# First projection of a fused transformer kernel: the first two weight units run together behind the norm's tiles, and GpSimd splits the second unit's weights right after the first's

## The reference

```python
def first_block(x, c, ...):
    x = layer_norm(x, ln_in_g, ln_in_b)
    c_act = jax.nn.silu(c)
    mod = c_act @ w_ada[l] + b_ada[l]            # 6 vectors of 1024
    sh1, sc1, gt1, sh2, sc2, gt2 = split(mod, 6)
    h = x * (1.0 + sc1) + sh1
    proj = h @ w_in[l]                           # 1024 x 1952
    q_c, kv_c, k_r, r_q, r_k, r_v, r_g = split(proj, IN_OFFSETS)
    a = mla_mixer(...); r = retention_mixer(...)
    y = concatenate([a, r]) @ w_out[l]
    ...                                          # norm, feed-forward, norm
```

## Time and profile before

| | |
|---|---|
| median of 3 runs | 2508.26 us (2506.33 to 2508.92) |
| the profiled execution | 2505.62 us |
| its span | 2503.8 us, so 1.8 us lie around it |
| mean granted clock of PE | 0.987 |
| busy PE, PEld | 95%, 75% of the span |
| busy DVE, POOL, ACT | 56%, 30%, 25% of the span |

### The profile page before, as it was taken

The page is one execution under the profiler, slowest core; times in us unless marked ns, Lnnn a source line. Parts: engine busy times, 40 slices in busy tenths (PEclk is TensorE's granted clock), DMA queues, the critical chain, the costliest instruction groups (busy, mean ns, idle before and its releaser), DMA issues.

```text
span 2503.8 us, 28798 instructions
## 1 busy us (share of the span) xinstructions
PE 2370.2 (95%) x11364; PEld 1889.9 (75%) x11364; DVE 1396.0 (56%) x1618; ACT 626.2 (25%) x943; POOL 761.7 (30%) x513
## 2 busy tenths in 40 slices
PE   6999889999999999999998799998998999999998
PEld 3777566667678888888886478886586788879977
DVE  7567764435633553454445879998528320337733
ACT  4012244432522112101123621213204210024520
POOL 1231330025562332333355122410246223240021
PEclk9999989999999999999999899999999999999999
DMA  6652000032242332333232121111132531110021
GB/s 234 200 183 79 22 20 9 9 119 84 62 119 75 111 96 83 98 107 99 80 106 78 31 101 48 34 42 51 42 118 84 170 86 45 50 34 18 2 93 76
DMA packets 227108, 200.42 MB, mean 80 GB/s; under 512 B 15040, under 2 KB 202816, under 8 KB 225968
## 3 DMA queue, kind: packets, MB, share of 16 engines
q1 hardware_dynamic: 221808, 172.06, 22.8%
q10 hardware_dynamic: 3840, 21.89, 2.2%
q0 software_dynamic: 1344, 4.91, 0.5%
HBM read 173.79 MB, written 17.83 MB: 77 GB/s over the span
## 4 chain that ended last, share of the span: by engine, by line
PE 77%; DVE 9%; issue 4%; ACT 4%; PEld 2%; DMA 1%; POOL 1%; PEldq 1%; SPq 0%; ACTq 0%; DVEq 0%; POOLq 0%
PE G L1741 28%; PE G L308 25%; PE M L3182 3%; PE G L1172 2%; PE M L315 2%; PE G L2678 2%; PE M L1776 1%; PE M L2680 1%; POOL WL L285 1%; PE M L3159 1%; PE M L1123 1%; PE M L1057 1%; DVE MMX L1389 1%; PE G L1152 1%; PEldq L3349 1%
## 5 line engine op out<-in xcount | busy, mean ns | idle before, releaser
L282 POOL TENSOR_SCALAR WH<-RAW 128x1024 fp32r<-128x1024 f32 (+1 forms) x156 | 134.1, 859 | 873.2 <-PE G L1741 453.9
L308 PE MATMUL G<-HH,WH 128*128 128x512 f32 x1024 | 321.0, 395 | 14.5 <-POOL WL L285 4.3
L308 PE MATMUL G<-HL,WH 128*128 128x512 f32 x1024 | 316.8, 391 | 0.0
L308 PE MATMUL G<-HH,WL 128*128 128x512 f32 x1024 | 316.5, 390 | 0.0
L285 POOL TENSOR_TENSOR WL<-RAW,WH 128x1024 fp32r<-128x1024 f32 (+1 forms) x156 | 302.1, 1936 | 13.0
L308 PEld LDWEIGHTS G<-HH,WH 128*128 128x128 f32 x1024 | 191.0, 189 | 59.1 <-issue 13.8
L308 PEld LDWEIGHTS G<-HH,WL 128*128 128x128 f32 x1024 | 193.1, 189 | 40.7
L308 PEld LDWEIGHTS G<-HL,WH 128*128 128x128 f32 x1024 | 193.0, 188 | 40.7
L1741 PE MATMUL G<-HH,WH 128*128 128x512 f32 x608 | 208.4, 394 | 4.7 <-POOL WL L285 4.7
L1741 PE MATMUL G<-HH,WL 128*128 128x512 f32 x608 | 205.5, 389 | 0.0
L1741 PE MATMUL G<-HL,WH 128*128 128x512 f32 x608 | 205.4, 389 | 0.0
(11 more groups left out here) (583 smaller groups left out, 4441.8 us busy)
## 6 DMA issues: line engine op xcount, KB each, us to landing
RAW<-in_w_ff SPq DMA_DIRECT2D x40, 512.0 KB, 3.8
RAW<-in_w_ff SPq DMA_DIRECT2D x80, 256.0 KB, 2.8
WVEC<-in_w_ada SPq DMA_DIRECT2D x24, 512.0 KB, 4.6
FVEC<-in_e_w_mod SPq DMA_DIRECT2D x24, 512.0 KB, 4.0
FVEC<-in_o_w_mod SPq DMA_DIRECT2D x24, 512.0 KB, 3.7
RAW<-in_o_w_in SPq DMA_DIRECT2D x24, 512.0 KB, 3.7
RAW<-in_e_w_in SPq DMA_DIRECT2D x20, 512.0 KB, 3.6
ADA<-in_w_ada SPq DMA_DIRECT2D x4, 2048.0 KB, 18.4
```

The lines of the kernel that those rows point to most:

```text
L282: pool.tensor_scalar(hi, raw, 1.0, 0.0, ALU.mult, ALU.add).then_inc(w_high, 1)
L308: m = pe.matmul(G[s][:, n * w:(n + 1) * w], part[s][:, k, :], acts[i][:, k, n * w:(n + 1) * w], start=first, stop=last)
```

## The change

The lead of "win" becomes a function of its own, `win_lead`: for each tile k it waits for `li_lo`, then issues the 6 matmuls of unit 0 into G0 and the 6 of unit 1 into G1. `win_pe` starts with unit 2. POOL waits for `ada_added` once, at unit 0, and splits unit 1's weights right after unit 0's; DVE's second increment of `ada_added` goes.

```diff
@@ start_dve
                 low(f)
                 low(f + 1)
-            dve.wait_ge(S("li_lo"), KT)
-            dve.sem_inc(ada_added, 1)
@@
+        def win_lead(pe):
+            u0 = info("win")["u0"]
+            for k in range(KT):
+                pe.wait_ge(S("li_lo"), k + 1)
+                for s in range(2):
+                    if k == 0:
+                        pe.wait_ge(w_split[s], u0 // 2 + 1)
+                        need(pe, unit_freed[s], u0 // 2)
+                    for part, a in ((WH, HH), (WH, HL), (WL, HH)):
+                        first, last = k == 0 and part is WH and a is HH, k == KT - 1 and part is WL
+                        for n in range(2):
+                            m = pe.matmul(G[s][:, half(n)], part[s][:, k, :], a[:, k, half(n)], start=first, stop=last)
+                    if k == KT - 1:
+                        m.then_inc(unit_done[s], 1)
+
         def win_pe(pe):
             for j in range(16):
-                if j:
+                if j >= 2:
                     gemm_unit(pe, j % 2, (u0 + j) // 2, SEQ, (HH, HL))
@@ win_pool
             for j in range(16):
-                if j < 2:
-                    pool.wait_ge(ada_added, j + 1)
+                if j == 0:
+                    pool.wait_ge(ada_added, 1)
                 split_one(pool, r0 + j, u0 + j, KT)
@@
-        stage("win", dict(lead=lead_in("win", SEQ, "li_lo"), act=win_act, pe=win_pe, dve=win_dve, sp_free=win_sp,
+        stage("win", dict(lead=win_lead, act=win_act, pe=win_pe, dve=win_dve, sp_free=win_sp,
```

## The result

The changed kernel took 2524.21 us (median of 4 runs, 2521.45 to 2525.88) against 2508.59 us for the kernel before in the same comparison: a ratio on record of 1.0052, 95% interval 1.0038 to 1.0066, so 9.5 to 16.6 us slower (13.0 in the middle). This ratio is not the quotient of the two medians, which is 1.0062 or 15.6 us; no run tells why, and the other ratios of this document differ from the quotient of their medians in the same way, by up to 0.0010. The forecast was 2519.5 in a range of 2514.5 to 2523.0. The direction, the place and the mechanism were right. The size was short: by the median 4.7 us, which puts the median 1.2 us above the range; by the ratio, put on the 2508.3 that the forecast started from, the time is 2521.3, which is 1.8 us above the forecast and inside the range.

The account below looks back on a forecast made before the run. TensorE, busy 95% of the 2503.8 us span, was taken as the bound. Gate 12.1, relief -1.4 and restart +0.8 made +11.5 us on 2508.3, so 2519.8, rounded down to 2519.5; range 2514.5 to 2523 us.

Parts of the forecast that it names:

- The mechanism: Gate behind the lead: opens after 96 matmuls instead of 48, delaying WVEC, unit 0's copy and unit 2; +12.1 us.
- The early split at the port: Start of the lead: GpSimd's split and VectorE's norm operations take turns, so TensorE starts 2.3 us late.
- the one played through: Order at the port: t32(0), GpSimd's first split operation, t32(2), GpSimd's subtraction, then low(0), ending at 52.4 us.
- The lead: Units 0 and 1 together, 96 matmuls: TensorE never waits after the first tile, and the lead ends at 76.4 us.
- The relief: Between gate and unit 2: unit 3's 512 KB load no longer travels with WVEC's, 1.4 us off the 11.86.
- The restart: Unit 2 after 10.6 us idle: lower clock loses 2.0 us; with unit 4's wait filled, net +0.8 us.
- After unit 4: Rest of the stage: copies wait for TensorE, not WVEC; loads, splits and stages follow TensorE's pace.
- The sum: Whole kernel: gate 12.1, less 1.4 relief, plus 0.8 restart, gives +11.5 us.
- VectorE keeps ahead at the port: Rival, chance 0.28: same gate, but the lead starts only 0.4 us late; +9.3 us, 2517.6 us.
- The gate costs nothing that counts: Rival, chance 0.05: WVEC's rows early or later waits swallow the delay; unit 2 waits for its split; no change, 2508.2.

Follow-up runs that it names:

- e2: Kernel before with unit 1 behind unit 0 in the lead, split late as before, nothing interleaved; ratio 1.0045 to the kernel before.
- e1: Kernel before with only the early split: GpSimd splits unit 1's weights right after unit 0's; ratio 1.0006 to the kernel before.
- e4: Changed kernel with the first two WVEC loads issued before the gate; ratio 1.0036 to the kernel before.
- e5: e12 plus the first two WVEC loads issued before the gate; ratio 1.0000 to the kernel before.
- e8: Changed kernel with the lead not interleaved, unit 0 over all eight tiles, then unit 1; ratio 1.0054 to the kernel before.
- e10: Changed kernel with 62 filling matmuls in front of unit 2, keeping TensorE busy through its wait; ratio 1.0041 to the kernel before.
- e12: e3 plus weights of unit j + 1 loaded ahead of unit j's spill and WVEC loads; ratio 1.0007 to the kernel before.
- e3: Changed kernel with VectorE copying units 0 and 1 out of PSUM before its first four row products; ratio 1.0050 to the kernel before.
- e9: Kernel before, unchanged, traced a second time; span 2509.0 us against 2503.8 in the first trace.
- e6: Kernel before with first two WVEC loads before the gate and unit j + 1's weights ahead of unit j's spill and WVEC loads; ratio 0.9984.
- e11: e6 plus VectorE copying unit 0 before its first two row products; ratio 0.9972 to the kernel before.

## Why the prediction was right, and where its size was off

*The mechanism.* Right. The copy of unit 0, behind WVEC behind the gate, is what unit 2 waits for, and e2 shows it with nothing else changed.

*The early split at the port.* Forecast 2.3 us, measured 2.0 to 2.1 (52.1 to 52.3 against 50.1 to 50.3) in e1, e4, e5, e8, e10 and e12. In the changed kernel's own trace the lead began 3.1 us late, and 2.9 in e3. In these two MODA's first operation ran at 46.65 and 46.53 instead of 45.36, so that L487 came just behind the start of GpSimd's WH (46.84 and 46.64), waited for it, and the subtraction went ahead of the first t32: another order than the one played through, and some 1.0 us dearer. The clock was at its lower level from 46 us in both. It was so too in e2 and e10, where MODA's operation ran at 46.26 and 46.19, L487 was through in 0.17 us, and the lead began at 50.27 (no early split) and 52.13. Whether the clock is low there is chance; that a delay of a few tenths costs 1.0 us comes with the early split.

*The lead.* Forecast to end at 76.4, measured 78.15 in that trace and 77.04 in e8. The loss to the clock at its start was set at 2.0 us; in the changed kernel it was 24.87 - 96 x 0.2276 = 3.0 us, so this term was mis-sized by 1.0 us. In the other traces with this lead the same loss was 1.6 us (e3), 1.8 (e10), 2.4 (e12) and 2.9 to 3.1 (e4, e5, e8). That TensorE had been slow since 46 us does not explain it: e3 and e10 had that too and lost least. Together with the later start the lead is the larger miss, 1.75 us.

*The relief.* The term that was most wrong by itself in this trace. I took 1.4 us off the 11.86 us between gate and unit 2, because unit 3's 512 KB no longer travelled with WVEC's rows. From POSI's issue at 78.28 to unit 2's start at 89.85 are 11.57 us: a relief of 0.3. The second WVEC load took 7.41 us to land, 7.04 before, although unit 3's weights were no longer in flight. From the gate's first issue to unit 2 were 11.8 us in e1, 11.1 in e8 and e10 and 10.3 in e2, all with unit 3's weights long loaded (at 64.05 in e2). So the relief was 0.1 to 1.5 us, 0.7 in the mean of the five; e2 had what I took. The stretch varies from trace to trace by as much as the whole term, and why it does is open.

*The restart.* 2.0 us gross and 0.8 net forecast; unit 2 took 12.8 us instead of 11.15, so 1.7 gross, and e10 against the changed kernel gives 0.5 net.

*After unit 4.* I let the rest of the stage follow TensorE's pace. From unit 4 to the stage's end are 138.3 us in the changed kernel and 138.8 before: right on average. What I missed is that the same queue has a second tight place, unit 7, and that a wait there can bring a low stretch of the clock with it, which cost up to 3 us (2.8 in e4). The length of the wait does not decide it: no low stretch followed 1.80 us (before, e10), 2.08 (changed kernel) and 2.50 (e8), but one came with 1.95 (e1), 2.47 (e9), 2.97 (e3), 3.44 (e4) and 3.85 (e2). The changed kernel's trace escaped it, so the 13.5 us hold some luck. Windows of e1 and of e8, both 2 to 3 us behind unit 7's start (columns as in rows 4):

```profile
...
137.00:138.00 1.00, 1.00 (x4) 0.81 (x3) 0.97 (x2) 0.00 (x0) 0.00 (x0) 0.50 1.04 374
...
```

```profile
...
150.00:151.00 1.00, 1.00 (x6) 0.84 (x5) 0.96 (x2) 0.00 (x0) 0.00 (x0) 1.00 0.79 261
...
```

*The sum.* 11.5 forecast, 13.5 at the stage's end between the first traces, 11.1 against the second trace of before, 13.0 by the ratio. The 15.6 us between the medians contain some chance of the first comparison, in which the kernel before had its median at 2508.59; in the later comparisons it was at 2509.2 to 2511.5. Up to unit 2 the parts add up: 0.8 us more at the port, 1.0 at the lead's clock and 1.1 less relief are the 2.9 us by which unit 2 came later than forecast (89.85 against 87.0). A restart 0.3 us cheaper and 0.5 us less between unit 4 and the stage's end take it to 13.5.

*The rivals.* "VectorE keeps ahead at the port" did not occur in any trace. "The gate costs nothing that counts" was wrong. Its number, no change, is the time of e5, but for another reason: e5's queue edits also remove waits that the kernel before has, and against a kernel before with such edits the change still costs some 5 us. GpSimd's split behind the pair, which the rival names, is one part of these (the 1.4 us above).

## What to carry to other kernels

A lead that a scheduler issues ahead of a stage's border is part of the border: before lengthening it, list every queue that waits there and what stands behind the waiting instruction, down to the weights of several units later. Freeing the wait that the trace names (e3) can be worth nothing if the next item of the same queue is as late: the copies alone changed nothing that the ratio shows, with the weights ahead as well (e12) the stage ended 9.7 us earlier than in the changed kernel. To price a change that carries repairs with it, give the same repairs to the kernel before (e5 against e6 and e11, not against before). And in a queue that is served in order, what TensorE needs next goes ahead of what only has to be done at some time: this alone made the kernel before faster.

## What the runs showed of the hardware

The instructions of GpSimd and VectorE took turns in every trace with the early split. In e1 two t32, WH, WL and the first two low parts took 6.7 us (46.55 to 53.23), where their lengths alone add up to 7.3, so they overlap at their edges only. In five of the eight (e1, e4, e5, e8, e12) the turn went to the one that had waited: WH 1.58 us between two t32, then WL, then low(0). In the changed kernel and in e3 WH ran first, beside the waiting L487, and WL before both t32; in e10 WH ran before the first t32. A copy from PSUM was not affected: in e11 the one at 64.00, beside GpSimd's split of unit 2 (64.11 to 67.63), took 1.22 us, as the others did alone. The Trainium skill (SBUF — State Buffer, section "Who interferes with whom") says that whichever of the two issues first keeps the shared pair for its whole instruction. The trace of e1 agrees, and shows besides that the one that waits comes in between two instructions of the other that stand back to back. The changed kernel's trace does not show it so plainly: t32 is recorded from 47.95 and WL from 47.98, and yet WL had its usual length (2.35 us) and t32 waited. A difference of 0.03 us in recorded starts is too small to build on.

The granted clock at the same instruction differed between executions of the same code: between 46 and 48 us it was at the upper level in both traces of before and at the lower in e2, whose code is the same up to there. Nor did the length of an idle time alone say what the clock did. After 2.50 us in front of unit 7 (e8) it stayed at 1.00, after 1.95 us (e1) and 2.47 us (e9) it fell when TensorE was already at work again, and in e4 (3.44 us) it fell during the wait. In front of unit 2 an idle time of 2.54 us was followed by a low stretch in e3 (80 to 83 us) and by none in e12 and e5.
